# Two token streams run one after the other at the borders between stages, with ScalarE applying LayerNorm's scale

## What is computed

```
for i in range(2):                       # layers of the first block
    m_lat = modulation(c, w_mod[i], b_mod[i]); m_ctx = modulation(c_ctx, ...)
    x_lat = layer_norm(ALPHA*x_lat + 0.5*gate*swiglu(x_lat*(1+scale)+shift), g, b)   # ffn
    x_ctx = the same with m_ctx
    y_lat, y_ctx = gmlp(h_lat), gmlp(h_ctx)   if i == 0   else   attention(h_lat, h_ctx)
    x_lat = layer_norm(ALPHA*x_lat + gate*y_lat, g, b)      # x_ctx too in layer 0
    x_lat = ffn sublayer                                    # x_ctx too in layer 0
```

## Time and profile before

| | |
|---|---|
| median of 3 runs | 3293.95 us (3284.95 to 3296.24) |
| the profiled execution's own time | 3284.43 us |
| its span in the profile | 3282.6 us |
| mean granted TensorE clock | 0.971 of 2.4 GHz |
| PE busy | 3111.3 us, 95% |
| DVE / ACT / POOL busy | 2034.7 / 983.5 / 654.8 us |

### The profile page before, as it was taken

How to read it: one execution, slowest core, us unless ns; L and a number is a source line. 1 busy time by engine, 2 the same in 40 slices (tenths; PEclk the granted TensorE clock), 3 DMA queues, 4 the chain that set the end, 5 groups by cost and what they waited for, 6 DMA issues and landing times.

```text
span 3282.6 us, 47123 instructions
## 1 busy us (share of the span) xinstructions
PE 3111.3 (95%) x19044; PEld 2748.7 (84%) x19044; DVE 2034.7 (62%) x2134; ACT 983.5 (30%) x1025; POOL 654.8 (20%) x640
## 2 busy tenths in 40 slices
PE   7999989999989999899998799999989999999899
PEld 3888879978868888688887599899878999988899
DVE  6653356757376443864428767586687757658764
ACT  1111223212122121211123444333533333343433
POOL 0210100114111010110100022131371304228110
PEclk9999999999999999999999999999999999999999
DMA  7533235322245333453333467596546859754464
GB/s 276 179 128 90 90 104 179 113 93 78 90 134 161 116 90 101 131 166 103 98 123 119 168 203 249 161 272 217 184 167 183 267 203 259 237 181 167 150 184 155
DMA packets 501652, 522.55 MB, mean 159 GB/s; under 512 B 15732, under 2 KB 433830, under 8 KB 501478
## 3 DMA queue, kind: packets, MB, share of 16 engines
q1 hardware_dynamic: 498536, 513.76, 48.5%
q0 software_dynamic: 2944, 6.32, 0.9%
HBM read 518.97 MB, written 1.05 MB: 158 GB/s over the span
## 4 chain that ended last, share of the span: by engine, by line
PE 81%; DVE 10%; ACT 3%; POOL 2%; issue 2%; DMA 2%; SPq 0%; DVEq 0%; ACTq 0%; POOLq 0%
PE ps L1967 29%; PE ps L2038 15%; PE ps L2122 15%; PE ps L2007 8%; PE ps L2146 6%; DVE wl L1144 2%; PE ps L1913 2%; ACT wh L773 1%; PE ps L2070 1%; DMA wraw<-in_ffn_w_out 1%; PE ps L2378 1%; POOL wst L743 1%; POOL lnp L749 1%; DVE x L1240 1%; PE ps L1953 1%
## 5 line engine op out<-in xcount | busy, mean ns | idle before, releaser
L1144 DVE TENSOR_TENSOR wl<-wraw,wh 128x2048 fp32r<-128x2048 f32 x341 | 847.4, 2485 | 646.4 <-ACT wh L773 639.8
L773 ACT ACTIVATE wh<-wraw 128x2048 fp32r<-128x2048 f32 x341 | 652.6, 1914 | 927.4 <-PE ps L2038 430.4
L1967 PE MATMUL ps<-xh,wh 128*128 128x512 f32 (+1 forms) x1600 | 598.4, 374 | 18.2 <-DVE xl L1196 15.5
L1967 PE MATMUL ps<-xh,wl 128*128 128x512 f32 (+1 forms) x1600 | 597.0, 373 | 0.0
L1967 PE MATMUL ps<-xl,wh 128*128 128x512 f32 (+1 forms) x1600 | 595.6, 372 | 0.0
L1117 DVE SCALAR_TENSOR_TENSOR acc<-mraw,svec,acc 128x1024 f32<-128x1024 f32 x329 | 427.1, 1321 | 20.8 <-DMA mraw<-in_w_mod 7.9
L2122 PE MATMUL ps<-xh,wh 128*128 128x258 f32 x1408 | 402.8, 286 | 5.3 <-DVE xl L1308 4.2
L2122 PE MATMUL ps<-xh,wl 128*128 128x258 f32 x1408 | 398.9, 283 | 0.0
L2122 PE MATMUL ps<-xl,wh 128*128 128x258 f32 x1408 | 398.5, 283 | 0.0
L617 POOL CAST hh<-ht 128x256 f32 (+1 forms) x176 | 116.7, 663 | 1283.7 <-DVE ht L1488 949.9
L1967 PEld LDWEIGHTS ps<-xh,wh 128*128 128x128 f32 x1600 | 305.7, 191 | 75.2 <-issue 19.4
(11 more groups left out here) (387 smaller groups left out, 4912.0 us busy)
## 6 DMA issues: line engine op xcount, KB each, us to landing
wraw<-in_ffn_w_in SPq DMA_DIRECT2D x352, 512.0 KB, 5.1
wraw<-in_ffn_w_out SPq DMA_DIRECT2D x176, 512.0 KB, 4.0
mraw<-in_ada_w SPq DMA_DIRECT2D x72, 1024.0 KB, 7.0
mraw<-in_w_mod SPq DMA_DIRECT2D x64, 1024.0 KB, 5.9
wraw<-in_gmlp_w_in SPq DMA_DIRECT2D x48, 512.0 KB, 4.4
wraw<-in_mix_w_in SPq DMA_DIRECT2D x48, 512.0 KB, 4.7
wraw<-in_gmlp_w_out SPq DMA_DIRECT2D x24, 512.0 KB, 3.9
first_w<-in_w_mod SPq DMA_DIRECT2D x8, 1024.0 KB, 13.4
```

Of the source, the lines that this page charges most:

```text
L773: act.activation(wh[:, slot], wraw[:, slot], ACT.Copy).then_inc(whi_done, 1)
L1144: dve.tensor_tensor(wl[:, slot], wraw[:, slot], wh[:, slot].bitcast(F32), ALU.subtract)\
L1967: m = pe.matmul(ps[:, bank, 0:width], a, b, start=k == p == 0, stop=k == KD - 1 and p == 2)
```

## The change

It has five parts.

1. **The last two out units as a pair** (`out_pair`, at the end of stages 0 to 3): PE runs both units for stream 0 and then both for stream 1, with the same 12 matmuls for a tile and unit as in `out_unit`. It waits for both units' weights before it begins.
2. **The border on DVE** (`border`, where `take(i)` is `take_y`'s step for token tile i): take tiles 0 and 1, LayerNorm statistics of stream 0, split unit u0, take tile 2, prepare stream 0, split unit u0+1, take tile 3, statistics of stream 1, prepare stream 1, gates.
3. **The scaling of LayerNorm on ACT** (`normalise_stream`), at borders into stages 1 to 4; DVE only works out an offset. ACT splits unit u0+1 ahead of it.
4. **The stage's beginning on PE** (`begin_two`, stages 0 to 4): transposes of stream 0 (banks 0 to 3), units u0 and u0+1 for stream 0 alone, transposes of stream 1 (banks 4 to 7), both units for stream 1, then the gate rows. No `keep_going` there.
5. **Tables**: the 12 modulation pieces of the next stage are taken from the third unit on and the columns come after the units with index 4 and 7 (`TWO_MODS`, `TWO_LOADS`, `TWO_COLUMNS`); these phases are written out instead of looped. In the second block's ffn the last piece and its columns come one unit later.

```diff
-FF_MODS = (2, 4, 6, 8, 10, 12, 14, 16, 18, 20, 22, 23)
+FF_MODS = (2, 4, 6, 8, 10, 12, 14, 16, 18, 20, 22, 24)
+TWO_MODS = (2, 2, 3, 4, 5, 5, 6, 7, 8, 8, 9, 10)
+TWO_LOADS = (3, 4, 5, 6, 6, 7, 8, 9, 9, 10, 11, 12)
+TWO_COLUMNS = (4, 7)
...
 @block.scalar
+            def normalise_stream(c):
+                n_normed[0] += 1
+                act.wait_ge(offset_ready, n_normed[0])
+                for t in range(TT):
+                    last = act.activation(x[:, c, t], x[:, c, t], ACT.Identity, bias=offset[:, t:t + 1], scale=rstd[:, t:t + 1])
+                last.then_inc(x_ready, 1)
...
                 if s["block"] == 1:
+                    if two(s):
+                        split_next(s["n_unit"])
                     for k, c in enumerate(s["streams"]):
+                        if two(s) and s["i"] > 0:
+                            normalise_stream(c)
                         prepare_half(s, k, c)
...
-                    phase(GM_UNITS, u0, 4, gelu)
+                    for i in range(GM_UNITS):
+                        if i:
+                            split_next(u0 + i)
+                        gelu(i, i % 2, 0)
...
 @block.vector
+            def layer_norm(c, scaled_by_act=False):
...
+                if scaled_by_act:
+                    dve.scalar_tensor_tensor(out=offset[:], in0=mv[:, :, 0], scalar=-1.0, in1=rstd[:],
+                                             op0=ALU.mult, op1=ALU.mult).then_inc(offset_ready, 1)
+                    return
...
+            def border(s, nxt, u, tiles, by):
...
+                take(0)
+                take(1)
+                steps.wait(added[1])
+                layer_norm(0, True)
+                split_next(nxt["n_unit"] - 1)
+                take(2)
+                prepare_half(nxt, 0, 0)
+                split_next(nxt["n_unit"])
+                take(3)
+                steps.wait(added[3])
+                layer_norm(1, True)
+                prepare_half(nxt, 1, 1)
+                gates(nxt)
...
+                        if two(s) and g == 0:
+                            for i in range(n):
+                                if i:
+                                    split_next(u0 + i)
+                                for sec, q in two_mods(i):
+                                    mod_unit(nxt, sec, q)
+                                evac(i, i % 2, 0)
+                                if i in TWO_COLUMNS:
+                                    mod_end(nxt, TWO_COLUMNS.index(i))
...
 @block.tensor
+            def begin_two(s, part):
+                u0, q0 = s["n_unit"], s["n_inq"]
+                for c in range(2):
+                    transposes(s, c)
+                    for i in range(2):
+                        pe.wait_ge(wlo_done, u0 + i + 2)
+                        pe.wait_ge(pair_free, q0 + i)
+                        m = part(i, c, 2 * (s["n_tr"] + c) + 1 if i == 0 else None)
+                        if c:
+                            m.then_inc(w_used, 1)
+                gate_rows(s)
...
+            def out_pair(u, chunk0, ready, halves=None):
+                for i in range(2):
+                    pe.wait_ge(wlo_done, u + i + 2)
+                ready()
+                for c in range(2):
+                    for i in range(2):
+                        slot = (u + i) % 2
+                        for t in range(TT * c, TT * c + TT):
+                            for kk in range(2):
...
+                            if i == 1 and t < 2 * TT - 1:
+                                m.then_inc(y_tile, 1)
+                        if c:
+                            m.then_inc(w_used, 1)
...
-                if s["block"] == 1:
+                if s["block"] == 1 and not two(s):
                     gate_rows(s)
-                    if s["i"]:
-                        keep_going(3, 16)
+                    keep_going(3, 16)
                     transposes(s)
...
-                    unit(0)
-                    unit(1)
+                    begin_two(s, key_part)
                     unit(2)
```

More of the change, by code:

```diff
@@ L212, in program @@
         rstd = sb("rstd", [P, TT])
+        offset = sb("offset", [P, TT])
         shift_col = sb("shift_col", [P, 2, 2])
@@ L415, in ff_mods, with two_mods, two @@
             return [(n // 4, n % 4) for n, at in enumerate(FF_MODS) if at == idx]
+        def two_mods(idx, table=TWO_MODS):
+            return [(n // 4, n % 4) for n, at in enumerate(table) if at == idx]
+        def two(s):
+            return s is not None and len(s["streams"]) == 2
         def sections(s, sec):
@@ L1418, in _ @@
                     factors(s)
-                if s["block"] == 1:
-                    for k, c in enumerate(s["streams"]):
-                        prepare_half(s, k, c)
+                if s["i"] == 0:
+                    prepare_half(s, 0, 0)
+                    split_next(s["n_unit"])
+                    prepare_half(s, 1, 1)
+                    gates(s)
+                elif s["block"] == 1 and not two(s):
+                    prepare_half(s, 0, 0)
                     gates(s)
@@ L1640, in _ @@
                     steps.link(op)
-                    unit(0, (0, 1))
+                    for n in (0, 1):
+                        mod_unit(nxt, 0, n)
                     k_part = nrm1[:, 16:24]
@@ L1896, in _ @@
                     unit(15)
-                if s["block"] == 1:
-                    layer_norm(s)
-                else:
+                if s["block"] == 1 and not two(nxt):
+                    layer_norm(0)
+                elif s["block"] == 2:
                     arrive(s, nxt)
@@ L2008, in token_tile, with features_of @@
                 return m
[L2010 to L2022 removed]
+            def features_of(slot, bank, r, c, ready=None):
+                for k in range(KD):
+                    if ready and r == 0 and k in (0, KD // 2):
+                        pe.wait_ge(pre_ready, ready + (k > 0))
+                    at, tokens = slice(k * CW + r * P, k * CW + (r + 1) * P), slice(c * T, (c + 1) * T)
+                    for p, (a, b) in enumerate(parts(wh[:, slot, at], wl[:, slot, at], now[0][:, k, tokens], now[1][:, k, tokens])):
+                        m = pe.matmul(ps[:, bank, tokens], a, b, start=k == p == 0, stop=k == KD - 1 and p == 2)
+                return m
@@ new lines, in out_pair @@
+            def out_pair(u, chunk0, ready, halves=None):
[7 more added lines that the diff above has]
+                            for kk in range(2):
+                                chunk = chunk0 + 2 * i + kk
+                                at = slice(chunk * 2 * T + t * P, chunk * 2 * T + (t + 1) * P)
+                                x_hi, x_lo = halves(chunk, t) if halves else (hh[:, at], hl[:, at])
+                                for half in range(2):
+                                    w = slice(kk * D + half * 512, kk * D + (half + 1) * 512)
+                                    for p, (b, a) in enumerate(parts(wh[:, slot, w], wl[:, slot, w], x_hi, x_lo)):
+                                        m = pe.matmul(ps[:, 2 * t + half], a, b, start=False, stop=i == kk == 1 and p == 2,
+                                                      skip_group_check=i == 0)
+                            if i == 1 and t < 2 * TT - 1:
+                                m.then_inc(y_tile, 1)
+                        if c:
+                            m.then_inc(w_used, 1)
@@ L2187, in _ @@
                             for r in range(2):
[L2188 removed]
+                                m = features(u1 % 2, 2 * pair + r, r, slice(0, 2 * T), 2 * T, False)
                             m.then_inc(w_used, 1)
```

250 lines of the change are left out of this document (152 added, 98 removed).

## The result

The changed kernel takes 3383.8 us (median of 4, 3380.7 to 3391.8) against 3289.5 us (median of 4) for the kernel before, measured together: ratio 1.029, 95% interval 1.026 to 1.032, or 94 us more. The forecast was 75 us more, and 3365 us. The profiled execution took 3383.6 us.

The account below looks back on a forecast made before the run. PE was taken as the bound, busy in 95% of the span. Losses of 11.4 (stage 0), 42.6 (three borders) and 21.2 (attention) sum to 75 us: 3360, put at 3365 for the median, range 3308 to 3398.

Parts of the forecast that it names:

- S: At a border, the moment at which the last two out units begin; zero point of the forecast's times.
- The pair: Last two out units: PE waits 4.3 us for the second unit's weights, then loses 1.7 us to low clock.
- The scaling bare on PE's path: After the pair, PE stands still 4.2 us for ACT's split and scaling; stream 0's transposes take 3.6 at low clock.
- The whole gain: Stage's start: the first matmul comes 6.5 us earlier than before, the only gain.
- Gate rows and their queue: Behind stream 1: gate rows 3.7 us, moved not removed; then PE waits 6.1 us for the third unit's split.
- Attention: Border into attention: DVE's work from gate to third unit's split follows bare; fourth unit's split at S + 101.4, 21.2 us more.
- A border before: Old border into stage 3: third unit starts at S + 72.3; after that unit both kernels run the same work.
- Costed at nothing: Away from the borders: DVE, ACT and POOL work, SP's loads, moved tables and relief of DVE, all taken as no cost.
- The clock stays up: Rival 1, chance 0.11: waits at the borders come as worked out but cost no clock; 31 us more, 3316.
- Only the front counts: Rival 2, chance 0.06: work behind the first matmul is covered, so the kernel is 35 us faster, 3249.
- DVE falls behind: Rival 3, chance 0.09: modulation pieces overload DVE in nine units; PE waits 3.7 us three times in four stages, 3405.
- No difference: Rival 4, chance 0.04: the six parts of a border cancel to within 2 us.

Follow-up runs that it names:

- Two runs that take it off the path: Changed kernel with ACT scaling stream 0 before splitting unit u0+1: 3365.7 us; changed kernel with LayerNorm's scaling back on DVE: 3358.5 us.
- the remedy: Changed kernel with scaling first, gate rows in the wait and a tile of 128 bytes: without the pair 3274.6 us, with it 3277.7 us.

## Why the prediction came out as it did

The sign and the mechanism were right, and the time lies in the range; the sum was 19 us short. That 3384 lies under the range's end of 3398 is in part luck: that end was made of larger clock losses and of the median's spread, and what filled it was mostly a pace that the prediction had at nothing. By its own steps, at the border into stage 3, as distances from S (the measured ones from the chain above):

| | forecast | measured |
|---|---|---|
| pair ends | 28.4 | 28.4 |
| transposes of stream 0 end | 36.2 | 36.4 |
| first matmul of the stage | 40.9 | 40.9 |
| second transposes begin | 55.2 | 54.4 |
| stream 1's halves end | 75.0 | 74.5 |
| gate rows end | 78.7 | 77.9 |
| third unit begins | 84.8 | 83.3 |
| third unit ends | 97.5 | 97.1 |

The last row is when ACT takes the unit, 1452.23, less 0.3. Before it was S + 72.3 + 11.0 = 83.3. So this border costs 13.8 us (13.9 in the measure of the table below), forecast 14.2. Errors cancel in it: the first halves lost 1.9 us to the clock and not 2.8 (13.46 us for two halves of 5.77), the second 2.3 and not 1.7 (13.79), DVE took 5.4 us from the gate rows to the split and not 6.1, and the clock behind that wait cost 2.7 us (13.87 for a unit of 11.20) and not 1.7.

The prediction carried this border over to the others. Measured in the same way, from ACT's split at S to the third unit's result (in attention to the end of the sixth unit's split; at the beginning of stage 0 from the start of the program), the five places are:

| place | forecast | measured |
|---|---|---|
| beginning of stage 0 | 11.4 | 10.5 |
| border into stage 1, gmlp | 14.2 | 16.8 |
| border into stage 2 | 14.2 | 14.9 |
| border into stage 3 | 14.2 | 13.9 |
| border into stage 4, attention | 21.2 | 23.4 |
| sum | 75 | 79.5 |

*The pair* (4.3 and 1.7 of clock): 4.37, and 24.06 us for 96 matmuls at the 233 ns of an out unit, so 1.7. Undoing it gave 26 us for 24. The clock's term isn't the same everywhere: behind a wait just as long, the pair ahead of gmlp took 25.52 us: 3.1 of clock, 1.4 more than the term, about half of what that border is over its forecast.

```profile
441.14 25.52 PE ps L2150 x96
```

*The scaling bare on PE's path* (4.2, and slow transposes of 3.6): 4.32 and 3.69. Two runs that take it off the path give 18 and 25 us. The scaling itself is 2.37 us, not 2.0.

*"The whole gain"*, the first matmul 6.5 us earlier: 40.9 against 47.4, as said, and worth nothing, as the rows behind it show.

*The wait of 4.7 paid twice*: 4.53 twice.

*Gate rows and their queue*: waits of 5.4 us and in attention 12.5, forecast 6.1 and 12.2 + 0.4 for the work from gate to split. The run that moves the gate rows gets 58 us back, the expectation was 50.

*Attention*: the fourth unit's split ends at 1878.43, S + 100.4 (S is 1778.06 there), forecast 101.4. But the unit's first 48 matmuls then take 8.32 us at a granted clock of 0.67, where they took 5.57 at 1.00; the forecast had no clock term there. From S to the end of the sixth unit's split are 117.8 us, before 94.4: 23.4 more, forecast 21.2. The splits behind it keep that distance.

*The beginning of stage 0*: the third unit ends at 112.2, before at 101.7: 10.5, forecast 11.4.

Together the five places are 79.5 us for the 75 forecast. The spans differ by 99.2. What failed is the premise in *A border before* that after the third unit both kernels run the same work, with no term for it under *Costed at nothing*: PE's instructions there are the same, their pace isn't. Ten input units took 109.88 us and now take 112.00. For stage 3 the account closes: 13.8 at its border, 9 units at 0.21 more, 2.1 for the ten and 0.5 in the out units are 18.3, and the stage is 18.3 us longer from S to S. The kernel before with 32 unused bytes, so with its tiles where the changed kernel has them, gives the price of that pace without the change: 14.7 us. Against that kernel the change costs 3383.8 - 3305.2 = 78.6 us, which is what the five places give in the traces, against the 75 forecast. So of the missing 19 us some 4 are border terms that came out too small (in gmlp and attention), and about 15 are a matter of where an added tile pushed the others.

What stays open: which address and which tile set the pace, and by what mechanism. It isn't `xh` modulo 64 or modulo 128; executions of one program differ in it too; and no run moved one tile alone. Of the difference of spans, 99.2 less 79.5 and less the 18.6 by which the span of the shifted kernel before (3301.2) exceeds that of the first profile leaves 1.1 us; two executions of the kernel before differ by 3.7 in the same measure.

The rivals. *The clock stays up* is refuted by the 0.50 behind the waits (it is the rival that the prediction means where it speaks of the second). What the prediction held for it, that 2.2 us of waiting cost nothing, is true of one border only: at the borders into stages 1 and 2 of the kernel before, the gate rows came behind the same 2.2 us and took 5.37 us, not 3.67, their first 3 us at 0.60 of the clock. *Only the front counts* is refuted in the form given, the third unit didn't come before the gates; but it names what the remedy does: with the gate rows inside the wait and the scaling first, what stands behind the first matmul is mostly covered, and the time (3275 to 3278 us) is no longer above that of the kernel before. *DVE falls behind* is refuted: DVE is idle in each input unit before its next split, by about 1.1 us (1.12 us before the split at 1465.87), and PE has no wait for `wl` in the units behind the third of the three two-stream ffn stages. *No difference* is refuted by the ratio.

## What to carry to other kernels

Splitting a stage's first units by stream brings its first matmul forward, but every step of the second stream that is queued behind the first stream's matmuls is paid a second time; count up to the first unit that runs the same in both orders, not to the first matmul. When a step moves to another engine, look at what stands ahead of it in that engine's queue: here 1.9 us of split made a relief of DVE into four waits of 4.3 us. Fill an unavoidable wait with the matmuls whose readers are needed soonest (58 us here), and before believing a difference of half a per cent, shift the memory layout by an unused tile and see whether it stays.

## What the runs showed of the hardware that was not expected

The pace of PE depends on where tiles lie in SBUF, at a granted clock of 1.00: with an unused tile of 32 bytes, 48 matmuls of 512 columns took 11.20 us in all 51 spacings, where most had been 10.99, and the kernel was 14.7 us (0.45%) slower; 128 bytes in the changed kernel made it 19 us faster; 64 bytes gave a third pace, 11.15, in half of the spacings. At one place the pace also differs from phase to phase and between two executions. That is 4 spacings of 0.21 us between the two profiles of the kernel before, so it doesn't explain the spread of 3283 to 3299 us that this kernel shows.

ACT takes 2.37 us to scale two tiles of 1024 with a bias and a scale for each partition, DVE 1.53.
